# Turning the raw rows as they land and putting the norm's factor in afterwards, with the recurrence's slabs in the order f, i, q, z

## The chip, the cores and the metric

One Trainium2 chip, one of its cores. The metric is the device time of one execution in microseconds (us). The kernel before takes 618.6 us, the median of 3 runs (618.35 to 620.24).

## The reference

A two-layer decoder trunk over 256 tokens of width 1024, all in float32. Each layer is a mixer and a cross attention, each with a residual. The change touches the first mixer, and of it the part A:

```
h = rms_norm(x, ev_norm) @ ev_w_in            # 8 parts of 1024 columns: aq, af, ai, bq, bk, bv, z (2048)
rms_norm(x, g) = x * rsqrt(mean(x*x) + 1e-6) * g
# part A, per head of 128, 8 heads, chunks of 32 tokens
f = lb + (1 - lb) * sigmoid(af);  k = 1 - f
b = cumsum(log f) within a chunk
q_dec = aq * exp(b);  k_inv = k * exp(-b);  k_end = k * exp(b_last - b)
o = causal(q_dec k_inv^T) ai + q_dec s_prev   # s_prev: the state carried from earlier chunks
y = head_rms_norm(o) * silu(z)
```

Part B is softmax attention on bq, bk and bv, with a rotary turn whose angles come from `positions`. Then come the output projection, the cross attention, and the second layer of the same build.

## The kernel before

**Slabs and quarters.** Every weight is cut into slabs of 1024 rows by 512 columns (2 MB). SP loads slab n into one of two raw buffers, once the slab before the last one has been split (`sp.wait_ge(lo_ready, 4 * (n - 1))`). A slab has four quarters. ACT rounds a quarter to `w_hi` and VectorE (DVE) takes the rest, `w_lo = raw - w_hi`. Each has a ring of four quarters. TensorE (PE) multiplies hi by hi, hi by lo and lo by hi: a quarter of a kind "F" slab is 24 matmuls of 256 columns (lines L1506 to L1508, the result has channels on partitions), a quarter of a kind "T" slab is 12 matmuls of 512 columns (L1524 to L1526, the result has tokens on partitions).

**The order is written out by hand in each engine's program.** The call `ahead(n, q)` on ACT and on DVE splits not quarter q of slab n but the one three further on:

```python
def ahead(n, q):
    n, q = divmod(4 * n + q + 3, 4)
    ...
    dve.wait_ge(hi_ready, 4 * n + q + 1)
    dve.tensor_tensor(ring_quarter(w_lo, n, q), raw_quarter(n, q), ...).then_inc(lo_ready, 1)
```

So `ahead(f, 0)` makes quarter 3 of slab f, and `ahead(f, 1)` quarter 0 of the slab after f. PE waits before each quarter until both halves of it are made. The engines take their instructions strictly in order, so a quarter whose `ahead` stands behind other work comes when that work is done.

**The start.** ACT squares the two row tiles of x (L494), DVE makes the mean's reciprocal (L931 to L935), ACT the root (L449), DVE multiplies the rows by it (`norm_rows`, L942), PE turns the result in 16 transposes of 128x128 (`turn_rows`, L1545), ACT writes `xT_hi` with the gain as a scale (L456), and DVE `xT_lo` (L949). The parameters (13 small DMAs into `prm_rows`) are turned by PE (L1554, L1555) and copied by ACT (L498) between them. All projections of the first mixer read `xT_hi` and `xT_lo`.

**Part A** runs twice, for g = 0 and g = 1 (4 heads each), `stage_a(g)`. Its slabs are in the order f, q, i, z (i is of kind T, the others of kind F). In words, for DVE in g = 1: split four quarters while f is multiplied; `forget(1, 0)` and `forget(1, 1)` on the sigmoids; `f_ready`; `ahead(q, 1)`; `gated_a(0)`, which is the end of group 0's output; `ahead(q, 2)` and `ahead(q, 3)`; then wait for ACT's logarithm and run the cumulative sum (L1114) and the chunk subtraction (L1121, `b_ready`); `ahead(i, 0)`, `ahead(i, 1)`; `k_inv` (L1128), `q_dec` (L1133), the carried halves (L1137, L1140). PE multiplies f, q, i, then waits for `k_inv` and `q_dec` (L1590), then z's quarter 0, the carried halves (L1598, L1602), z's 1 and 2, the outputs (L1614), z's 3. In g = 1 a `mean_square_a(0)` (L1571, four matmuls) stands behind the first quarter of f; the second one stands behind the first quarter of stage B.

In g = 0, DVE also computes the rotary angles (`angles`, L1016 to L1039) among the splits, ACT the sine (L537), and DVE sets its signs (`sign_trig`, L1068 and L1069). In g = 1, GpSimd (POOL) makes `y_lo` of group 0 (L379) when ACT has written `y_hi`.

Of the kernel before, what the change touches and what calls it, by code (L numbers as in the profile page):

```python
# [9 lines left out]
I32 = mybir.dt.int32  # L10
# [39 lines left out]
for _g in range(2):  # L50
    SLABS += [("A", "f", "F", _g), ("A", "q", "F", _g), ("A", "i", "T", _g), ("A", "z", "F", _g)]
# [29 lines left out]
def hybrid_trunk(nc, I, out):  # L81
    with ExitStack() as ctx:
# [50 lines left out]
        fgain = wview(1)  # L133
        kx = scan_mask[:, :].rearrange("p (h t) -> p h t", h=4)
# [13 lines left out]
        mem_landed = sem("mem_landed")  # L148
        prm_landed = sem("prm_landed")
# [13 lines left out]
        trig_ready = sem("trig_ready")  # L163
        sumsq = sem("sumsq")
# [126 lines left out]
        def _(sp):  # L291
# [6 lines left out]
            first_quarter(0)  # L298
            for name, rows in PARAM_ROWS:
# [6 lines left out]
                sp.dma_start(prm_rows[r - P * t:r - P * t + rows, t, :], src).then_inc(prm_landed, 16)  # L306
            for q in range(1, 4):
                first_quarter(q)
            for n in range(1, NSLAB):
                if n == 2:  # L310
                    sp.dma_start(const[:], I["shape_constants"]).then_inc(pos_landed, 16)
                    sp.dma_start(W[:, 3, 0:S].bitcast(I32), I["positions"].broadcast_to([P, S])).then_inc(pos_landed, 16)
# [26 lines left out]
        def _(pool):  # L339
# [3 lines left out]
                               pattern=[[-1, P]], channel_multiplier=1).then_inc(masks_ready, 1)  # L343
# [11 lines left out]
            pool.memset(avg[:], 1.0 / P)  # L355
# [51 lines left out]

            keys_carried(0)
# [12 lines left out]
        def _(act):  # L421
# [61 lines left out]

            def y_high(i):
# [5 lines left out]
            act.preload_act_table(ACT.Sqrt)  # L490
            for t in range(T):
# [4 lines left out]
            ahead(-1, 1)  # L496
            act.wait_ge(prm_turned, 1)
            act.activation(prm[:], proj[0][:, 0:N_ROWS], ACT.Copy).then_inc(prm_ready, 1)  # L498
            act.drain()
            xT_high(0, 0, "ev_norm", 0)  # L500
            ahead(-1, 2)
            ahead(-1, 3)
# [16 lines left out]

            def stage_a(g):  # L520
                f, q, i, z = (slab("A", c, g) for c in "fqiz")
                ahead(f, 0)
# [4 lines left out]
                filled(act, f, 0)  # L527
                act.activation(W[:, 0, 0:512], bank(f, 0)[:], ACT.Sigmoid).then_inc(f_sig, 1)
                act.drain().then_inc(free_of(f, 0), 1)
                ahead(f, 3)  # L530
                ahead(q, 0)
                filled(act, f, 1)
                act.activation(W[:, 0, 512:1024], bank(f, 1)[:], ACT.Sigmoid).then_inc(f_sig, 1)
                act.drain().then_inc(free_of(f, 1), 1)
                if g == 0:
# [3 lines left out]
                ahead(q, 1)  # L539
                if g:  # L540
# [12 lines left out]
                ahead(i, 1)  # L553
                ahead(i, 2)
                ahead(i, 3)
                ahead(z, 0)
                v_rows(i)
                ahead(z, 1)
                ahead(z, 2)
                ahead(z, 3)  # L560
# [357 lines left out]
        def _(dve):  # L918
# [63 lines left out]
            ahead(-1, 2)  # L982
            ahead(-1, 3)

            lg = prm[:, PARAM_AT["hgrn_lb_logits"]:PARAM_AT["hgrn_lb_logits"] + 3 * KC].rearrange(
# [869 lines left out]
```

## Time and profile before

| | |
|---|---|
| median of 3 runs | 618.6 us |
| profiled execution | 618.5 us, of which the span from first to last instruction is 616.8 us |
| busy: PE, DVE, ACT, POOL | 586.1, 413.2, 374.3, 43.4 us |
| share of the span that ends last, by engine | PE 66%, DVE 14%, ACT 9% |

Times are microseconds from the first instruction. In a timeline row the first number is the start, the second the time to the end of a merged group, and "x16" the number of instructions in it; in brackets stands how long the engine was idle before it and what released it.

### The profile page before, as it was taken

Reading aid. Unit: us, or ns where it says so; the run is one execution under the profiler, and the core shown is the slowest. Engines: PE = TensorE matmul, PEld = TensorE weight load, DVE = VectorE, ACT = ScalarE, POOL = GpSimd, SP = SyncE. Lnnn points to the kernel's source line nnn. Section 1 sums busy time; section 2 is a strip of 40 time slices with the busy share of each in tenths; the row PEclk is TensorE's granted clock in tenths of the full one; section 3 lists DMA queues with packets and bytes.
Section 4 is the critical chain, followed back from the end, with each engine's and each line's share of the span. In section 5 each row is a group of like instructions: output and inputs, shape, how many; then the busy total and the mean of one; then the engine's idle time right before and its main releaser. Section 6 shows DMA issues by size and latency. Waiting matters only on the chain.

```text
span 616.8 us, 9596 instructions
## 1 busy us (share of the span) xinstructions
PE 586.1 (95%) x3858; PEld 534.1 (87%) x3858; DVE 413.2 (67%) x618; ACT 374.3 (61%) x553; POOL 43.4 (7%) x45
## 2 busy tenths in 40 slices
PE   3999998999999999999999999998989999999984
PEld 3998997999899898889988999997879897888973
DVE  3987378537965884566557782979946962776554
ACT  5864485257267665646657648598357547566662
POOL 4001003001001000100000001131101000100000
PEclk9999999999999999999999999999999999999998
DMA  8747454445535463563336463333333473256101
GB/s 244 248 144 218 141 181 133 140 137 205 159 115 167 150 230 137 180 228 138 137 138 204 156 247 144 137 137 138 136 137 137 145 265 128 101 202 250 38 1 69
DMA packets 51872, 97.83 MB, mean 159 GB/s; under 512 B 1236, under 2 KB 7668, under 8 KB 51828
## 3 DMA queue, kind: packets, MB, share of 16 engines
q1 hardware_dynamic: 51828, 97.22, 46.4%
q8 instruction: 31, 0.51, 0.3%
q14 instruction: 13, 0.11, 0.0%
HBM read 96.16 MB, written 1.05 MB: 158 GB/s over the span
## 4 chain that ended last, share of the span: by engine, by line
PE 66%; DVE 14%; ACT 9%; DVEq 5%; issue 3%; ACTq 2%; DMA 1%; SPq 0%
PE proj L1506 10%; PE proj L1507 10%; PE proj L1508 10%; PE proj L1524 8%; PE proj L1526 8%; PE proj L1525 8%; DVE w_lo L925 5%; PE head L1614 3%; ACT w_hi L434 3%; PE head L1703 1%; ACT xT_hi L456 1%; DVEq L1115 1%; DVE work L1114 1%; DMA x_residual<-in_x_dram 1%; DVE xT_lo L949 1%
## 5 line engine op out<-in xcount | busy, mean ns | idle before, releaser
L925 DVE TENSOR_TENSOR w_lo<-raw_weights,w_hi 128x1024 fp32r<-128x1024 f32 x176 | 221.9, 1274 | 144.2 <-ACT w_hi L434 142.6
L434 ACT ACTIVATE w_hi<-raw_weights 128x1024 fp32r<-128x1024 f32 x176 | 184.1, 1057 | 136.5 <-PE proj L1508 72.5
L1506 PE MATMUL proj<-xT_hi,w_hi 128*128 128x256 f32 x768 | 223.7, 291 | 3.3 <-DVE xT_lo L949 1.7
L1507 PE MATMUL proj<-xT_lo,w_hi 128*128 128x256 f32 x768 | 218.0, 284 | 0.0
L1508 PE MATMUL proj<-xT_hi,w_lo 128*128 128x256 f32 x768 | 218.0, 284 | 0.0
L1506 PEld LDWEIGHTS proj<-xT_hi,w_hi 128*128 128x128 f32 x768 | 148.0, 193 | 6.6 <-issue 5.8
L1507 PEld LDWEIGHTS proj<-xT_lo,w_hi 128*128 128x128 f32 x768 | 148.1, 193 | 1.4 <-issue 1.2
L1508 PEld LDWEIGHTS proj<-xT_hi,w_lo 128*128 128x128 f32 x768 | 147.9, 193 | 0.0
L1524 PE MATMUL proj<-w_hi,y_hi 128*128 128x512 f32 x192 | 76.2, 397 | 0.0
L1526 PE MATMUL proj<-w_lo,y_hi 128*128 128x512 f32 x192 | 74.8, 390 | 0.0
L1525 PE MATMUL proj<-w_hi,y_lo 128*128 128x512 f32 x192 | 74.8, 389 | 0.0
L1524 PEld LDWEIGHTS proj<-w_hi,y_hi 128*128 128x128 f32 x192 | 36.1, 188 | 8.3 <-issue 0.6
L1526 PEld LDWEIGHTS proj<-w_lo,y_hi 128*128 128x128 f32 x192 | 36.0, 188 | 7.6
L1525 PEld LDWEIGHTS proj<-w_hi,y_lo 128*128 128x128 f32 x192 | 36.1, 188 | 7.4 <-issue 0.2
L1524 PE MATMUL proj<-w_hi,xT_hi 128*128 128x512 f32 x96 | 37.9, 394 | 2.3 <-DVE w_lo L925 2.2
L1525 PE MATMUL proj<-w_hi,xT_lo 128*128 128x512 f32 x96 | 37.4, 390 | 0.0
L1526 PE MATMUL proj<-w_lo,xT_hi 128*128 128x512 f32 x96 | 37.4, 390 | 0.0
L379 POOL TENSOR_TENSOR y_lo<-work,y_hi 128x1024 fp32r<-128x1024 f32 x7 | 17.7, 2531 | 274.1 <-ACT y_hi L487 274.1
L1524 PEld LDWEIGHTS proj<-w_hi,xT_hi 128*128 128x128 f32 x96 | 18.0, 188 | 7.1 <-issue 2.6
L1526 PEld LDWEIGHTS proj<-w_lo,xT_hi 128*128 128x128 f32 x96 | 18.0, 188 | 3.9
L1525 PEld LDWEIGHTS proj<-w_hi,xT_lo 128*128 128x128 f32 x96 | 18.1, 188 | 3.4
L949 DVE SCALAR_TENSOR_TENSOR xT_lo<-head,prm,xT_hi 128x256 fp32r<-128x256 f32 x32 | 12.9, 475 | 8.2 <-ACT xT_hi L456 8.2
(237 smaller groups left out, 684.5 us busy)
## 6 DMA issues: line engine op xcount, KB each, us to landing
raw_weights<-in_ev_w_in_dram SPq DMA_DIRECT2D x15, 2048.0 KB, 8.5
raw_weights<-in_od_w_in_dram SPq DMA_DIRECT2D x12, 2048.0 KB, 8.5
raw_weights<-in_ev_w_out_dram SPq DMA_DIRECT2D x4, 2048.0 KB, 8.1
raw_weights<-in_xa_wkv_dram SPq DMA_DIRECT2D x4, 2048.0 KB, 8.4
raw_weights<-in_od_w_out_dram SPq DMA_DIRECT2D x4, 2048.0 KB, 7.7
raw_weights<-in_xa_wq_dram SPq DMA_DIRECT2D x2, 2048.0 KB, 9.0
raw_weights<-in_xa_wo_dram SPq DMA_DIRECT2D x2, 2048.0 KB, 8.3
raw_weights<-in_ev_w_in_dram SPq DMA_DIRECT2D x4, 512.0 KB, 5.6
```

Source lines behind the costliest of these rows:

```text
L379: pool.tensor_tensor(y_lo[:, 4 * G:4 * G + 4, :], y_src(i), y_hi[:, 4 * G:4 * G + 4, :].bitcast(F32), ALU.subtract).then_inc(y_lo_ready, 1)
L434: act.activation(ring_quarter(w_hi, n, q), raw_quarter(n, q), ACT.Copy).then_inc(hi_ready, 1)
L456: act.activation(xT_hi[:, k, :], head[k // 2][:, S * (k % 2):S * (k % 2) + S], ACT.Copy, scale=param(gain, gk + k)).then_inc(xT_hi_ready, 1)
L925: dve.tensor_tensor(ring_quarter(w_lo, n, q), raw_quarter(n, q), ring_quarter(w_hi, n, q).bitcast(F32), ALU.subtract).then_inc(lo_ready, 1)
L949: dve.scalar_tensor_tensor(out=xT_lo[:, k, :], in0=head[k // 2][:, S * (k % 2):S * (k % 2) + S], scalar=param(gain, gk + k), in1=xT_hi[:, ...
L1506: pe.matmul(dst, wh[:, k, :], x_hi[:, k, :], start=(k == 0), stop=False)
L1507: pe.matmul(dst, wh[:, k, :], x_lo[:, k, :], start=False, stop=False)
L1508: last = pe.matmul(dst, wl[:, k, :], x_hi[:, k, :], start=False, stop=(k == KC - 1))
L1524: pe.matmul(dst, x_hi[:, k0 + k, tok], wh[:, k, :], start=first and k == 0, stop=False)
L1525: pe.matmul(dst, x_lo[:, k0 + k, tok], wh[:, k, :], start=False, stop=False)
L1526: last = pe.matmul(dst, x_hi[:, k0 + k, tok], wl[:, k, :], start=False, stop=final and k == 1)
L1614: last = pe.matmul(dst[:, a:a + w], v_sb[:, t, P * h:P * h + P], src, start=(j == 0), stop=(j == len(spans) - 1), skip_group_check=True)
```

## The change

1. The order of the slabs in part A becomes f, i, q, z.
2. PE turns the raw rows of x as they land, after 6 matmuls of the identity by itself. ACT and DVE write the turned rows times the gain into `y_hi` and `y_lo` (`raw_high`, `raw_low`). The first two slabs (f and i of group 0) are multiplied with these. Their results lack the norm's factor. DVE puts it in for f (`scaled_f`, by a row of factors that PE spreads with a matmul of `avg` and a diagonal), ACT for i (`scaled_v_rows`, a scale for each token).
3. POOL splits the second quarter of the first slab (`second_low`) and makes the normed rows (`first_rows`). PE turns these behind the f slab, and `xT_hi` and `xT_lo` are written behind that, for the q slab and later ones.
4. SP loads the gain alone behind the first quarter, then the three other quarters, then the 12 other small rows.
5. Angles, sine and signs move from g = 0 to g = 1, and their scratch space from `work` to `memT`.
6. In `stage_a`, z's quarter 0 comes ahead of the L1590 group, and the outputs come behind z's quarter 3.

The diff's core (DVE and PE; the ACT side follows the same order):

```diff
-    SLABS += [("A", "f", "F", _g), ("A", "q", "F", _g), ("A", "i", "T", _g), ("A", "z", "F", _g)]
+    SLABS += [("A", "f", "F", _g), ("A", "i", "T", _g), ("A", "q", "F", _g), ("A", "z", "F", _g)]
...
             first_quarter(0)
+            small_rows(*PARAM_ROWS[0], gain_landed)
             for q in range(1, 4):
                 first_quarter(q)
+            for name, rows in PARAM_ROWS[1:]:
+                small_rows(name, rows, prm_landed)
...
+            def second_low():
+                pool.wait_ge(hi_ready, 2)
+                pool.tensor_tensor(ring_quarter(w_lo, 0, 1), raw_quarter(0, 1), ...).then_inc(second_lo, 1)
+            def first_rows():
+                pool.wait_ge(rstd_ready, 1)
+                for c in range(2):
+                    for t in range(T):
+                        last = pool.tensor_scalar(mem_rows[:, t, 512 * c:512 * c + 512], ...)
+                    last.then_inc(normed, 1)
...
+            act.preload_act_table(ACT.Sqrt)
+            square_row(0)
+            act.wait_ge(prm_turned, 1)
+            act.activation(prm[:, 0:KC], proj[2][:, 0:KC], ACT.Copy).then_inc(prm_ready, 1)
+            ahead(-1, 1)
+            act.drain()
+            raw_high(range(0, 4))
+            ahead(-1, 2)
+            raw_high(range(4, 8))
+            ahead(-1, 3)
+            square_row(1)
+            act.wait_ge(prm_turned, 2)
+            act.activation(prm[:, KC:], proj[2][:, KC:N_ROWS], ACT.Copy).then_inc(prm_ready, 1)
             root(0)
+            ahead(slab("A", "f", 0), 0)
+            act.wait_ge(rstd_psum, 1)
+            act.activation(rstd_row, proj[3][:, 0:S], ACT.Copy).then_inc(rstd_copied, 1)
...
-            norm_rows(0, x_sb, W[:, 0:2, :])
             ahead(-1, 1)
             dve.wait_ge(prm_ready, 1)
-            xT_low(0, "ev_norm", 0)
-            ahead(-1, 2)
-            ahead(-1, 3)
+            raw_low(range(KC))
+            dve.wait_ge(second_lo, 1)
+            dve.wait_ge(hi_ready, 3)
+            dve.tensor_tensor(ring_quarter(w_lo, 0, 2), raw_quarter(0, 2), ...).then_inc(lo_ready, 2)
+            rstd(0)
...
+            last.then_inc(diag_ready, 1)
+            ahead(slab("A", "f", 0), 0)
+            dve.wait_ge(prm_ready, 2)
...
             def angles():
...
-                ahead(slab("A", "f", 0), 2)
+                ahead(slab("A", "f", 1), 2)
...
-                ahead(slab("A", "f", 0), 3)
+                ahead(slab("A", "f", 1), 3)
...
             def stage_a(g):
+                if g:
+                    ahead(f, 0)
+                    ahead(f, 1)
+                    angles()
+                    forget(g, 0)
+                    ahead(i, 0)
+                else:
+                    ahead(f, 1)
+                    scaled_f(f, 0)
+                    ahead(f, 2)
+                    forget(g, 0)
+                    ahead(f, 3)
+                    scaled_f(f, 1)
+                    ahead(i, 0)
+                forget(g, 1)
...
+                ahead(i, 1)
+                if g:
+                    gated_a(0)
+                    sign_trig()
                 else:
-                    sign_trig()
-                ahead(q, 2)
-                ahead(q, 3)
+                    xT_low(0, "ev_norm", 0)
                 dve.wait_ge(lnf_ready, g + 1)
...
                 last.then_inc(b_ready, 1)
-                ahead(i, 0)
-                ahead(i, 1)
+                ahead(i, 2)
+                ahead(i, 3)
                 dve.wait_ge(exps_ready, 3 * g + 3)
                 dve.tensor_tensor(wview(0), wview(1), wview(0), ALU.mult).then_inc(kinv_ready, 1)
+                ahead(q, 0)
+                ahead(q, 1)
+                ahead(q, 2)
...
+            warm_up(6)
+            for t in range(T):
+                pe.wait_ge(x_landed[t], 16)
+                for k in range(KC):
+                    last = pe.transpose(head[k // 2][...], x_sb[:, t, P * k:P * k + P], ident[:])
+                    if t and k % 2:
+                        last.then_inc(x_turned, 1)
+                if t == 0:
+                    pe.wait_ge(gain_landed, 16)
+                    pe.transpose(proj[2][:, 0:KC], prm_rows[0:KC, 0, :], ident[0:KC, 0:KC]).then_inc(prm_turned, 1)
+            def first_slab(n):
+                quarter_f(n, 0, y_hi, y_lo, raw_x=True)
+                pe.wait_ge(prm_ready, 1)
+                pe.wait_ge(prm_landed, 16 * (len(PARAM_ROWS) - 1))
+                pe.transpose(proj[2][:, 0:P], prm_rows[:, 0, :], ident[:])
...
+                quarter_f(n, 1, y_hi, y_lo)
+                pe.wait_ge(diag_ready, 1)
+                pe.matmul(proj[3][:, 0:S], avg[:], memT[:, 5, :], start=True, stop=True).then_inc(rstd_psum, 1)
+                slab_f(n, [2, 3], x=(y_hi, y_lo))
+                turn_rows(mem_rows, 0)
+                pe.wait_ge(prm_ready, 2)
+                pe.wait_ge(rstd_copied, 1)
...
+                if g:
+                    slab_f(f, [0])
                     mean_square_a(0)
+                    slab_f(f, [1, 2, 3])
+                    slab_t(i)
+                    slab_f(q)
+                else:
+                    first_slab(f)
+                    slab_t(i, x=(y_hi, y_lo))
+                    slab_f(q, norm=0)
+                slab_f(z, [0])
```

## Rows read from the trace of the kernel before

**Rows 1.** Waits of PE in the first 130 us: total, times, longest.
```profile
PE head L1590 <- issue: 1.6, 1, 1.6
PE head L1590 <- DVE work L1133: 0.4, 1, 0.4
```
**Rows 2.** Timeline of PE, from the first slab to stage B.
```profile
18.09 0.32 PE L1506 MATMUL proj<-xT_hi,w_hi 128*128 128x256 f32 x1
...
71.49 1.88 PE L1571 MATMUL head<-work,avg 128*128 128x512 f32 x4
72.80 0.68 PE L1506 MATMUL proj<-xT_hi,w_hi 128*128 128x256 f32 x1
...
93.34 0.40 PE L1524 MATMUL proj<-w_hi,xT_hi 128*128 128x512 f32 x1
...
106.03 2.02 PE L1590 MATMUL head<-work 128*128 128x128 f32 x16 [1.61 <-issue]
...
127.04 1.88 PE L1571 MATMUL head<-work,avg 128*128 128x512 f32 x4
```
**Rows 3.** Timeline of all engines in the first 22 us.
```profile
1.71 0.43 SPq L296 DMA_DIRECT2D raw_weights<-in_ev_w_in_dram  x1
...
6.98 2.54 SPq L296 DMA_DIRECT2D raw_weights<-in_ev_w_in_dram  x3
...
12.13 0.30 ACT L498 ACTIVATE prm<-proj 128x160 f32<-128x160 f32 x1 [3.48 <-PE proj L1555]
12.52 3.03 ACT L456 ACTIVATE xT_hi<-head,prm 128x256 fp32r<-128x256 f32 x8
...
13.48 3.22 DVE L949 SCALAR_TENSOR_TENSOR xT_lo<-head,prm,xT_hi 128x256 fp32r<-128x256 f32 x8 [2.86 <-ACT xT_hi L456]
...
14.11 0.55 PE L1506 MATMUL proj<-xT_hi,w_hi 128*128 128x256 f32 x1 [0.97 <-DVE xT_lo L949]
...
18.89 0.16 DVE L987 TENSOR_TENSOR lbp<-prm 128x8 f32<-128x8 f32 x1
...
21.23 2.36 DVE L925 TENSOR_TENSOR w_lo<-raw_weights,w_hi 128x1024 fp32r<-128x1024 f32 x2
```
**Rows 4.** DMA issues between 1.7 and 2.0 us: size, us to landing.
```profile
raw_weights<-in_ev_w_in_dram SPq DMA_DIRECT2D x1, 512.0 KB, 5.6
```
**Rows 5.** Timeline of PE at the transposes of the memory's rows.
```profile
205.08 1.91 PE L1545 MATMUL head<-ident,shared_rows 128*128 128x128 f32 x16
206.74 0.47 PE L1524 MATMUL proj<-w_hi,xT_hi 128*128 128x512 f32 x1
```
**Rows 6.** Timeline of DVE: the angles in group 0, and group 1.
```profile
23.51 0.29 DVE L1016 CAST work<-work 128x256 f32<-128x256 int32 x1
...
32.53 0.73 DVE L1075 TENSOR_SCALAR work<-work,lbp 128x256 f32<-128x256 f32 x2
...
88.34 1.66 DVE L1083 SCALAR_TENSOR_TENSOR work<-head,prm,work 128x256 f32<-128x256 f32 x4 [1.06 <-ACT work L518]
...
91.22 2.36 DVE L925 TENSOR_TENSOR w_lo<-raw_weights,w_hi 128x1024 fp32r<-128x1024 f32 x2
...
99.14 1.22 DVE L925 TENSOR_TENSOR w_lo<-raw_weights,w_hi 128x1024 fp32r<-128x1024 f32 x1
```
**Rows 7.** Timeline of ACT: the sine in group 0, and the roots in group 1.
```profile
32.65 1.06 ACT L537 ACTIVATE trig<-trig 128x1024 f32<-128x1024 f32 x1 [2.05 <-DVE trig L1039]
...
35.02 2.01 ACT L434 ACTIVATE w_hi<-raw_weights 128x1024 fp32r<-128x1024 f32 x2
...
85.93 1.25 ACT L516 ACTIVATE work<-head,stats 128x512 f32<-128x512 f32 x2
```
**Rows 8.** Two lines by themselves: ns min/median/max, first and last start.
```profile
L1114 DVE TENSOR_TENSOR_SCAN work<-scan_mask,work x2: 2284/3388/4493, 40.1 to 93.5; 128x1024 f32<-128x1024 f32 x2
L379 POOL TENSOR_TENSOR y_lo<-work,y_hi x7: 2404/2415/3088, 92.8 to 529.7; 128x1024 fp32r<-128x1024 f32 x7
```
**Rows 9.** Windows at the end: length, busy of PE, PEld, DVE, ACT, POOL, granted clock, DMA.
```profile
606.00:610.00 4.00, 2.69 (x12) 1.88 (x10) 1.83 (x4) 1.41 (x5) 0.00 (x0) 1.00 0.00 0
612.00:614.00 2.00, 0.00 (x0) 0.00 (x0) 0.66 (x2) 1.16 (x2) 0.00 (x0) 0.52 0.43 158
```

More of the change, by code:

```diff
@@ L133, in hybrid_trunk @@
         fgain = wview(1)
+        rstd_row = memT[:, 4, :]
         kx = scan_mask[:, :].rearrange("p (h t) -> p h t", h=4)
@@ L296, in first_quarter, with small_rows @@
                 sp.dma_start(raw_quarter(0, q), dram_slab(0)[:, :, P * q:P * q + P]).then_inc(first_landed[q], 16)
-            first_quarter(0)
-            for name, rows in PARAM_ROWS:
+            def small_rows(name, rows, landed):
                 src = I[name]
@@ L482, in v_rows, with scaled_v_rows, raw_high @@
                     copy_bank(n, t, v_sb[:, t, :], v_ready)
+            def scaled_v_rows(n):
+                for t in range(T):
+                    filled(act, n, t)
+                    act.activation(v_sb[:, t, :], bank(n, t)[:], ACT.Copy, scale=st[:, 6 + t:7 + t]).then_inc(v_ready, 1)
+                    act.drain().then_inc(free_of(n, t), 1)
+            def raw_high(ks):
+                for k in ks:
+                    if k % 2 == 0:
+                        act.wait_ge(x_turned, k // 2 + 1)
+                    act.activation(y_hi[:, k, :], head[k // 2][:, S * (k % 2):S * (k % 2) + S], ACT.Copy,
+                                   scale=param("ev_norm", k)).then_inc(raw_hi_ready, 1)
             def y_high(i):
@@ L487, in y_high, with square_row @@
                 act.activation(y_hi[:, 4 * G:4 * G + 4, :], y_src(i), ACT.Copy).then_inc(y_hi_ready, 1)
-            act.preload_act_table(ACT.Sqrt)
-            for t in range(T):
+            def square_row(t):
                 act.wait_ge(x_landed[t], 16)
@@ L526, in stage_a @@
                 ahead(f, 2)
[L527 to L529 removed]
+                forget_gate(f, g, 0)
                 ahead(f, 3)
[L531 to L535, printed above, removed]
+                ahead(i, 0)
+                forget_gate(f, g, 1)
+                if g:
                     act.wait_ge(angles_ready, 1)
@@ L552, in stage_a @@
                 act.activation(wview(3), wview(2), ACT.Exp).then_inc(exps_ready, 1)
-                ahead(i, 1)
[L554 to L560, printed above, removed]
+                ahead(q, 0)
+                if g:
+                    v_rows(i)
+                else:
+                    scaled_v_rows(i)
+                for j in range(1, 4):
+                    ahead(q, j)
+                for j in range(4):
+                    ahead(z, j)
                 squares_a(g)
@@ L977, in _, with raw_low @@
             dve.drain()
-            norm_rows(0, x_sb, W[:, 0:2, :])
+            def raw_low(ks):
+                for k in ks:
+                    dve.wait_ge(raw_hi_ready, k - k % 2 + 2)
+                    dve.scalar_tensor_tensor(out=y_lo[:, k, :], in0=head[k // 2][:, S * (k % 2):S * (k % 2) + S],
+                                             scalar=param("ev_norm", k), in1=y_hi[:, k, :].bitcast(F32),
+                                             op0=ALU.mult, op1=ALU.subtract).then_inc(raw_lo_ready, 1)
             ahead(-1, 1)
             dve.wait_ge(prm_ready, 1)
-            xT_low(0, "ev_norm", 0)
-            ahead(-1, 2)
-            ahead(-1, 3)
+            raw_low(range(KC))
+            dve.wait_ge(second_lo, 1)
+            dve.wait_ge(hi_ready, 3)
+            dve.tensor_tensor(ring_quarter(w_lo, 0, 2), raw_quarter(0, 2), ring_quarter(w_hi, 0, 2).bitcast(F32),
+                              ALU.subtract).then_inc(lo_ready, 2)
+            rstd(0)
+            diag = memT[:, 5, :]
+            dve.wait_ge(masks_ready, 1)
+            for t in range(T):
+                last = dve.tensor_scalar(diag[:, P * t:P * t + P], ident[:], st[:, 6 + t:7 + t], float(P),
+                                         ALU.mult, ALU.mult)
+            last.then_inc(diag_ready, 1)
+            ahead(slab("A", "f", 0), 0)
+            dve.wait_ge(prm_ready, 2)
             lg = prm[:, PARAM_AT["hgrn_lb_logits"]:PARAM_AT["hgrn_lb_logits"] + 3 * KC].rearrange(
@@ L1134, in stage_a @@
                                       ALU.mult).then_inc(qdec_ready, 1)
+                    if u == 0:
+                        ahead(q, 3)
                 dve.drain().then_inc(free_of(q, 0), 1)
@@ L1607, in stage_a @@
                 out_a(g)
-                slab_f(z, [3])
             def values_out(h, spans):
```

111 lines of the change are left out of this document (67 added, 44 removed).

## The prediction

> **What bounds the kernel now.** I read the waits of PE first, then its timeline, then DVE and ACT beside it. From the first matmul of a slab at 14.11 [rows 3] PE runs almost without a gap: in the first 130 us its waits behind that are the two ahead of L1590, 0.4 us in group 0 and 1.6 in group 1 [rows 1]. So the end is set by three things: when PE gets its first slab, how much it has to multiply, and where it must wait. An edit on another engine counts only through these.
>
> Lengths used below. A quarter of kind F takes (93.34 - 72.80) / 7 = 2.93 us, the four matmuls of L1571 take 72.80 - 71.49 = 1.3, and the T slab 106.03 - 1.61 - 93.34 = 11.1 [rows 2]. From one L1571 group to the next, 71.49 to 127.04, it is 55.55 us [rows 2]: the length of group 1. ACT splits a quarter in 1.0 [rows 7], DVE in 1.2 [rows 6].
>
> **Part 1: the start and group 0.** Before, squares, root, normed rows, 16 transposes and the parameters all stand ahead of the first matmul at 14.11. After, the first quarter of weights has landed at 1.71 + 5.6 = 7.3 [rows 3, 4], and x was there earlier, since ACT was squaring it. The gain is issued right behind that quarter, and I take it to land with it. Its turn and copy cost 0.3 each (the copy of all parameters took 0.30 [rows 3]): 7.9. ACT's split brings 8.9, DVE's 10.1, and from the first `raw_low` to the first matmul it is 0.63, as from 13.48 to 14.11 [rows 3]. PE starts at about 10.7, so 3.4 us sooner. ACT makes the eight turned pieces at 3.03 / 8 = 0.38 with a split (1.0) in their middle, and DVE follows by about 13.9. PE at its lower clock needs 8 x 0.64 = 5.1 us for the quarter, so this pacing costs some 0.1.
>
> PE gets new work in exchange. The 16 transposes of the normed rows now stand behind the f slab: 206.74 - 205.08 = 1.7 [rows 5]. The two transposes of the parameters cost 0.4 and the `avg` matmul 0.2 (a half of one of L1571's, 1.3 / 4). The wait of 0.4 at L1590 [rows 1] goes, since z's quarter 0 (2.93) now covers it. Sum: -3.4 + 0.1 + 1.7 + 0.4 + 0.2 - 0.4 = -1.4.
>
> DVE must keep up with that. PE asks for quarter 1 of q at 10.7 + 4.7 (quarter 0, partly at the low clock) + 0.4 + 2.93 + 0.2 + 5.9 + 1.7 + 11.1 + 2.93 = 40.5. DVE makes it behind `b_ready`. It has split f's last quarter at about 19.2 (the q2 rounding ends at 14.1, then the second square, 1.2, the root and its steps, 1.0, and a split on each engine). From there it has the lower bound's operations, 2.3 (18.89 to 21.23 [rows 3]), and 0.6 more for ACT's table; five splits, 6.0; two `scaled_f`, 1.3; `forget` twice, 0.73 each [rows 6], and `f_ready`, 0.8; `xT_low`, 3.2 [rows 3]; the scan, 2.3 at its shortest [rows 8], and what follows it, 1.2; then the split itself, 1.2. With 1 us of waits for ACT this gives 19.2 + 21.3 = 40.5. Both arrive together, so I take 0.1 for a slip: **-1.3**, between -2.2 (PE starts a microsecond sooner) and -0.3 (DVE is a microsecond late). Slab 1 is issued later by the 12 small rows, at about 12 instead of 9.6, but the three quarters ahead of it now go out behind the first one instead of at 6.98 [rows 3], so I have it land at 20 as before, and ACT needs it at 21. POOL's split and its normed rows lie beside PE's first slab.
>
> **Part 2: group 1, where the new order puts a split behind the scan.** I count from the first L1571 group, 71.49 = 0. Before, `b_ready` comes at 99.14 - 71.49 = 27.65, and the first split behind it [rows 6] is the last quarter of i, which PE wants at about 30. The two quarters ahead of it were split at 91.22, ahead of the scan [rows 6]. The change takes these two `ahead` calls out from ahead of the scan and puts them behind `b_ready`. Now the last split ahead of the scan is quarter 0 of q. PE comes to quarter 1 of q at 1.3 + 3 x 2.93 + 11.1 + 2.93 = 24.1.
>
> When is `b_ready`? The two splits less (2.3) are made up by what moved in. Angles cost 32.53 - 23.51 - two splits = 6.7 us of DVE [rows 6]. They start behind `ahead(f, 1)`, at about 4, and with two splits in them end at 13. Sine and table take 35.02 - 32.65 = 2.4 of ACT [rows 7], a split 1.0, so the roots start at 16.4 instead of 85.93 - 71.49 = 14.4 [rows 7]. `gated_a` starts as much later, 18.9 instead of 16.85, takes 2.9 [rows 6] and ends at 21.8; signs 0.6; the scan starts at 22.4, where it was 22.0 [rows 8]. From scan to `b_ready` it was 5.6 (93.5 to 99.14), with POOL's `y_lo` beside the scan. Kept so, `b_ready` is at 28.0 and the quarter at 29.2. PE waits 29.2 - 24.1 = 5.1 us. Behind that the splits come every 1.2 us and PE takes 2.93 for each, so there is no second wait. `q_dec` is done 0.7 behind the q slab, and z's quarter 0 covers it: the 1.6 at L1590 goes. Group 1: +5.1 - 1.6 = **+3.5**. With the scan at 2.3, as in group 0 [rows 8], `b_ready` is 2.2 sooner, and it is +1.3. That is the lower bound. The upper one is +4.2, if the sine's load shifts the chain by 0.7 more.
>
> The clock may add to it. After its last matmuls, at about 608.7, PE had nothing, and in 612 to 614 the granted clock was 0.52 [rows 9]: it fell after some 3.4 us. The wait of 5.1 is longer. At the start it took until 18.09 [rows 2] to get from the first slab's matmul at the low level (1.2 GHz) to the high one (2.4): 4 us, in which a matmul took 0.21 instead of 0.12, so 1.7 us lost. I take 1.0 between 0 and 1.7, because the fall may come too late in the gap to happen. The Trainium skill (TensorE: Matmul & The Clock Gate, What's actually happening) says as well that idleness closes the gate and only sustained activity opens it again; by it the full 1.7 would be due whenever the gap closes the gate.
>
> Group 1's other moves lie under cover: `memT` as scratch costs nothing, the outputs behind z's last quarter move ACT's squares by 2.9, still ahead of the next L1571, and stages behind it are as before.
>
> **Sum** against the profiled 618.5 (span 616.8 and 1.7 around it): 618.5 - 1.3 + 3.5 + 1.0 = 621.7. The median is 0.1 above the profiled run: **621.8**.
>
> **The rivals.**
> - *The scan escapes POOL.* It starts before `y_lo` does, since ACT must first write `y_hi` (1.0), and takes 2.3, and the subtraction goes on before POOL takes its turn. For it speaks group 0's 2.28 [rows 8]; against it, that the subtraction has to come through as well. The wait is 2.9, too short for the clock to fall: 618.6 - 1.3 + 1.3 = 618.6, no change. The Trainium skill (SBUF — State Buffer, Who interferes with whom) says that DVE with two SBUF inputs and a GpSimd instruction that reads SBUF exclude each other, and the first to start keeps the ports for its whole length; the 4.49 against 2.28 agrees. By it the scan would run free, and POOL's 2.4 would then hold up the subtraction instead, which comes to the forecast again; only if the subtraction got in first is it this rival. Chance 0.17.
> - *Faster: no wait in group 1.* One mechanism: the chain to `b_ready` in group 1 runs ahead, because it now has two splits less. It decides if `b_ready` is there by 22.9, 5.1 sooner than I have it. Then -1.3 - 1.6: 615.7. Against it: the roots' row and `gated_a` alone reach 21.8. A much sooner start would also do (another 2 us). Chance 0.12.
> - *The start gives nothing back.* The gain lands late, or DVE's chain in group 0 (scaled copies, `xT_low`, blocked operations beside POOL's normed rows) is 2 us later than counted, so q's quarter 1 waits in group 0 too: 621.8 + 1.6 = 623.4. Both meet at 40.5, which speaks for it. Chance 0.12.
>
> **How the numbers follow.** The forecast has 0.59, with its own range 620.2 (clock stays up) to 623.6 (full clock loss, upper bounds). The range of all cases leaves out most of the 0.12 below and a little above: 617.0 to 624.3. Within 0.3% is 616.7 to 620.5, about what a measurement of this kernel can tell from no change. Faster: 0.12 and a tail of the first rival, 0.13. Same: most of the first rival and the forecast's low end, 0.25. Slower: 0.62.
>
> **What would show it.** In the profile after: the first slab matmul near 10.7; L1571 groups 59 to 60 us apart instead of 55.55; PE's longest wait behind the start at a quarter of q in group 1, released by DVE's `w_lo`; matmuls of 0.21 us behind it; no wait at the matmuls of L1590. I am wrong if the split of q's quarter 1 is made before PE has done quarter 0, which a `b_ready` 5 us sooner would do, or if the start is worth more than 3.4 us to PE.

## The result: 1% slower, more than forecast

The changed kernel takes 625.5 us (median of 4 runs, 624.5 to 626.1) against 618.65 us for the kernel before in the same rounds: ratio 1.0094, 95% interval 1.0077 to 1.0112. (Ratios here are those on record; they are close to, but not exactly, the quotient of the two medians, which is 1.011 here.) The forecast was 621.8 with a range up to 624.3, so the sign was right and the size was not: 3.7 us are missing. The profiled execution took 624.5 us with a span of 622.8, where before had 618.5 and 616.8.

The two longest waits of PE in the first 135 us of the changed kernel (total, times, longest); two more, of 1.8 and 1.1 us, also stand ahead of the first slab's work. They answer to [rows 1]:

```profile
PE proj L1613 <- DVE w_lo L993: 5.1, 1, 5.1
PE proj L1674 <- DMA prm_rows<-in_ev_norm_dram: 2.3, 1, 2.3
```

Both waits of [rows 1] are gone, and one of 5.1 has come. (The one of 2.3, for the gain, lies ahead of the first slab.) PE's timeline shows where (the counterpart of [rows 2]; L1613 to L1615 are a quarter of kind F, L1703 is the group that was L1571):

```profile
11.12 0.55 PE L1613 MATMUL proj<-y_hi,w_hi 128*128 128x256 f32 x1 [1.06 <-DVE y_lo L1050]
...
70.59 1.88 PE L1703 MATMUL head<-work,avg 128*128 128x512 f32 x4
...
94.59 0.28 PE L1615 MATMUL proj<-xT_hi,w_lo 128*128 128x256 f32 x1
99.94 0.55 PE L1613 MATMUL proj<-xT_hi,w_hi 128*128 128x256 f32 x1 [5.08 <-DVE w_lo L993]
100.30 0.42 PE L1614 MATMUL proj<-xT_lo,w_hi 128*128 128x256 f32 x1
100.51 0.41 PE L1615 MATMUL proj<-xT_hi,w_lo 128*128 128x256 f32 x1
...
103.70 0.28 PE L1615 MATMUL proj<-xT_hi,w_lo 128*128 128x256 f32 x1
103.82 0.28 PE L1613 MATMUL proj<-xT_hi,w_hi 128*128 128x256 f32 x1
...
131.23 1.88 PE L1703 MATMUL head<-work,avg 128*128 128x512 f32 x4
```

The start and group 0 give 71.49 - 70.59 = 0.9 back. Group 1 takes 131.23 - 70.59 = 60.64 us instead of 55.55: +5.1. Behind the wait the matmuls start 0.21 us apart up to 103.7, and 0.12 from there on. That makes +4.2 at 131 us.

The rest comes 320 us later, in work that the change does not touch. PE's timeline of stage D of the second layer, after and before:

```profile
454.42 4.53 PE L1750 MATMUL head<-shared_rows,v_rows 128*128 128x256 f32 x16 [2.31 <-DVE shared_rows L1523]
458.70 0.36 PE L1613 MATMUL proj<-xT_hi,w_hi 128*128 128x256 f32 x1
```

```profile
450.10 2.86 PE L1614 MATMUL head<-shared_rows,v_rows 128*128 128x256 f32 x16 [2.30 <-DVE shared_rows L1421]
452.71 0.36 PE L1506 MATMUL proj<-xT_hi,w_hi 128*128 128x256 f32 x1
```

The same 16 matmuls behind the same wait of 2.3 us take 4.53 us in place of 2.86, and the next slab starts 6.0 later than before instead of 4.3. Windows of the changed kernel over both places (length; busy of PE, PEld, DVE, ACT, POOL; granted clock; DMA):

```profile
95.00:100.00 5.00, 0.06 (x1) 0.09 (x1) 4.85 (x8) 1.30 (x3) 2.65 (x1) 0.68 0.00 0
100.00:103.00 3.00, 3.00 (x14) 3.00 (x15) 3.00 (x3) 2.85 (x4) 2.10 (x2) 0.50 0.00 0
104.00:105.00 1.00, 1.00 (x10) 1.00 (x10) 0.78 (x1) 0.46 (x2) 1.00 (x2) 1.00 0.66 205
450.00:454.00 4.00, 2.11 (x18) 1.90 (x16) 4.00 (x5) 1.43 (x3) 2.26 (x1) 1.00 0.00 0
454.00:456.00 2.00, 1.58 (x7) 1.38 (x8) 1.42 (x2) 1.77 (x2) 0.00 (x0) 0.81 0.77 182
456.00:458.00 2.00, 2.00 (x8) 1.78 (x7) 1.22 (x2) 0.60 (x1) 0.00 (x0) 0.50 1.04 403
```

The granted clock is 0.50 (1.2 GHz) behind both waits. In group 1 it fell within the wait: a mean of 0.68 over 95 to 100 puts the fall near 96.8, 2.0 us after PE's last matmul, and it was up again near 103.7. In stage D it was still 1.00 through the wait and fell some 0.8 us after PE had gone to work again. So the profiled difference is -0.9 + 5.1 + 1.7 = 5.9, against 6.0 of span.

DVE in group 1 of the changed kernel shows what the 5.1 are made of (the counterpart of [rows 6]; L1213 is the scan, L1220 the subtraction of `b_ready`), with POOL's `y_lo` below it:

```profile
89.83 1.66 DVE L1170 SCALAR_TENSOR_TENSOR work<-head,prm,work 128x256 f32<-128x256 f32 x4 [1.06 <-ACT work L577]
...
93.23 2.28 DVE L1213 TENSOR_TENSOR_SCAN work<-scan_mask,work 128x1024 f32<-128x1024 f32 x1
95.59 2.10 DVE L1217 COPY chunk_sum<-work 128x32 f32<-128x32 f32 x1
97.77 0.90 DVE L1220 TENSOR_TENSOR work<-work,chunk_sum 128x128 f32<-128x128 f32 x4
98.58 2.35 DVE L993 TENSOR_TENSOR w_lo<-raw_weights,w_hi 128x1024 fp32r<-128x1024 f32 x2
```

```profile
93.96 3.69 POOL L395 TENSOR_TENSOR y_lo<-work,y_hi 128x1024 fp32r<-128x1024 f32 x1 [46.10 <-ACT y_hi L536]
```

### The profile page after: what moved, and what is told of

Same layout as the page of the kernel before. It is cut to its first block, busy times and chain, and to the rows that moved or that the text cites. A ratio compares the mean times of both kernels' runs of the same rounds, so it can differ in the third digit from the quotient of the medians.

```text
span 622.8 us, 9685 instructions
## 1 busy us (share of the span) xinstructions
PE 593.7 (95%) x3889; PEld 541.3 (87%) x3889; DVE 418.2 (67%) x625; ACT 377.9 (61%) x563; POOL 58.0 (9%) x50
## 4 chain that ended last, share of the span: by engine, by line
PE 77%; DVE 9%; ACT 6%; DVEq 2%; ACTq 2%; issue 2%; DMA 1%; SPq 0%
PE proj L1613 13%; PE proj L1614 13%; PE proj L1615 13%; PE proj L1631 9%; PE proj L1633 9%; PE proj L1632 9%; PE head L1750 4%; DVE w_lo L993 3%; ACT w_hi L468 2%; PE head L1839 1%; DMA prm_rows<-in_ev_norm_dram 1%; PE head L1652 1%; ACT xT_hi L490 1%; DVE v_rows L1444 1%; PE head L1727 1%
## 5 line engine op out<-in xcount | busy, mean ns | idle before, releaser
L1613 PE MATMUL proj<-xT_hi,w_hi 128*128 128x256 f32 x736 | 214.8, 292 | 7.5 <-DVE w_lo L993 6.8
L1614 PE MATMUL proj<-xT_lo,w_hi 128*128 128x256 f32 x736 | 208.8, 284 | 0.0
L1615 PE MATMUL proj<-xT_hi,w_lo 128*128 128x256 f32 x736 | 208.8, 284 | 0.0
L1613 PEld LDWEIGHTS proj<-xT_hi,w_hi 128*128 128x128 f32 x736 | 141.7, 193 | 11.1 <-issue 10.3
L1614 PEld LDWEIGHTS proj<-xT_lo,w_hi 128*128 128x128 f32 x736 | 141.9, 193 | 1.5 <-issue 1.2
L1615 PEld LDWEIGHTS proj<-xT_hi,w_lo 128*128 128x128 f32 x736 | 141.7, 193 | 0.0
L1631 PE MATMUL proj<-w_hi,y_hi 128*128 128x512 f32 x208 | 82.5, 397 | 0.0
L1631 PE MATMUL proj<-w_hi,xT_hi 128*128 128x512 f32 x80 | 31.6, 395 | 2.2 <-DVE w_lo L993 2.2
L1613 PE MATMUL proj<-y_hi,w_hi 128*128 128x256 f32 x96 | 28.5, 296 | 1.1 <-DVE y_lo L1050 1.1
L1614 PE MATMUL proj<-y_lo,w_hi 128*128 128x256 f32 x96 | 27.9, 291 | 0.0
L1615 PE MATMUL proj<-y_hi,w_lo 128*128 128x256 f32 x96 | 27.8, 290 | 0.0
L1613 PEld LDWEIGHTS proj<-y_hi,w_hi 128*128 128x128 f32 x96 | 19.2, 200 | 1.8 <-issue 1.7
```

The lines of the kernel that those rows point to most:

```text
L1613: pe.matmul(dst, wh[:, k, :], x_hi[:, k, :], start=(k == 0), stop=False)
L1614: pe.matmul(dst, wh[:, k, :], x_lo[:, k, :], start=False, stop=False)
L1615: last = pe.matmul(dst, wl[:, k, :], x_hi[:, k, :], start=False, stop=(k == KC - 1))
L1631: pe.matmul(dst, x_hi[:, k0 + k, tok], wh[:, k, :], start=first and k == 0, stop=False)
```

## The experiments

Groups and times are those of each kernel's profiled execution. "Fill" is a multiplication of the identity by itself into a bank that the next group overwrites; it changes no result.

**Turn the chain round (scan_first).** Group 1 runs logarithm, scan and subtraction right behind the forget gates; the roots, `gated_a`, the signs and `y_high` come behind.

```diff
@@ DVE, g = 1
                 ahead(i, 1)
-                gated_a(0)
-                sign_trig()
                 dve.wait_ge(lnf_ready, g + 1)
                 ... scan, b_ready
                 ahead(i, 2)
                 ahead(i, 3)
+                gated_a(0)
                 ... k_inv
                 ahead(q, 0)
                 ahead(q, 1)
                 ahead(q, 2)
+                sign_trig()
```

> The changed kernel, with group 1's chain turned round: logarithm, scan and subtraction come straight behind the forget gates, and the roots, group 0's gated output and the signs come behind them, so the splits of q's quarters 1 and 2 are made by about 93.5 and 94.7 where PE wants them at 94.7 and 97.6. Theory A (the split behind the scan makes the wait): no wait of PE in group 1, the two L1703 groups 54.0 us apart instead of 60.6, about 616.2 us, or 617.9 if the clock still falls at the wait of 2.3 us in stage D. Rival B (the later cost is not this wait, but the new order or the new start as such): at least 621. Rival C (the clock's falls have nothing to do with the long wait): the clock still falls once in group 1.

Measured 619.0 us (12 runs, 617.0 to 621.3), ratio 0.9997 (0.9982 to 1.0013). Its DVE timeline in group 1:

```profile
88.66 2.29 DVE L1210 TENSOR_TENSOR_SCAN work<-scan_mask,work 128x1024 f32<-128x1024 f32 x1
91.02 0.19 DVE L1214 COPY chunk_sum<-work 128x32 f32<-128x32 f32 x1
91.28 0.90 DVE L1217 TENSOR_TENSOR work<-work,chunk_sum 128x128 f32<-128x128 f32 x4
92.10 2.35 DVE L993 TENSOR_TENSOR w_lo<-raw_weights,w_hi 128x1024 fp32r<-128x1024 f32 x2
```

The quarter is split 6.5 us sooner, PE does not wait for it, the clock stays up in group 1, and the L1703 groups are 125.65 - 70.57 = 55.08 apart (a wait of 1.15 at L1727, the former L1590, is left). The whole loss of group 1 came from that one wait. The copy takes 0.19 with POOL idle and 2.10 beside it. The time is 1.1 above the 617.9 expected with a fall in stage D (the profile has that fall): the wait of 1.15 at L1727 was not foreseen. The 12 runs lie 4.3 us apart, so they stand on several steps.

**Fill the wait (filled_gap, filled_22).** 44, then 22 fills stand between quarters 0 and 1 of q in group 1, so that PE is busy while it waits.

```diff
-                    slab_f(q)
+                    slab_f(q, [0])
+                    pe.wait_ge(y_ready, 1)
+                    for _ in range(44):      # 22 in filled_22
+                        pe.matmul(head[3][:, 0:P], ident[:], ident[:], start=True, stop=True)
+                    slab_f(q, [1, 2, 3])
```

> The changed kernel with 44 multiplications of the identity by itself put into PE's wait of 5.1 us ahead of q's quarter 1 in group 1; their result is used nowhere. Theory A (the wait costs 3.5 net, and the clock's fall in it 1.6 more): the quarter still starts at about 99.9, but the matmuls behind it come every 0.12 us at once, and the time is 1.6 us less than the changed kernel's. Rival (the slow matmuls do not lie on the path, since DVE's splits set the pace there): no change. Either way the wait of 2.3 us in stage D comes at another distance from the start, and its fall of the clock may or may not come again.

> As the run with 44 multiplications in the wait, but with 22, since each takes two steps of the array and 44 of them ran 4.4 us past the end of the wait. Theory A: they end about when the split does, the clock stays up in group 1, the two L1703 groups are 59.0 us apart (60.6 in the changed kernel), and the time is 1.6 us under the changed kernel's. Rival (the clock's fall there costs nothing on the path): 60.6 apart, no change.

44 were too many: they held PE until 103.87, and the kernel took 627.0 us (6 runs, ratio 1.0114), 1.5 over the changed kernel and not 1.6 under it as expected. But the clock did not fall in group 1, and from the first matmul behind the fill to the next L1703 group it was 133.54 - 103.87 = 29.67, where the changed kernel has 131.23 - 99.94 = 31.29. With 22 the wait is just covered: 623.2 us (4 runs, 622.8 to 623.5), ratio 1.0063, and

```profile
70.95 1.88 PE L1703 MATMUL head<-work,avg 128*128 128x512 f32 x4
...
129.97 1.88 PE L1703 MATMUL head<-work,avg 128*128 128x512 f32 x4
```

59.02 apart in place of 60.64. Both give the same price for the fall in group 1: 1.6 us. The low clock lasted about 6.8 us there, of which 3.1 fell into the wait and cost nothing.

**Old order in group 1 (old_order_g1).** Slabs f, q, i, z there; the splits stay where the change put them, for the slabs in this sequence. On ACT `v_rows` of i also moves back, behind one more split.

```diff
-for _g in range(2):
-    SLABS += [("A", "f", "F", _g), ("A", "i", "T", _g), ("A", "q", "F", _g), ("A", "z", "F", _g)]
+SLABS += [("A", "f", "F", 0), ("A", "i", "T", 0), ("A", "q", "F", 0), ("A", "z", "F", 0)]
+SLABS += [("A", "f", "F", 1), ("A", "q", "F", 1), ("A", "i", "T", 1), ("A", "z", "F", 1)]
```

> The changed kernel, but in group 1 with the slabs in the order of before (f, q, i, z), while the splits keep their new places: two of them behind the chunk subtraction. Theory A (the place of the splits decides, not the order of the slabs): PE waits at quarter 1 of the third slab (now i) about 5 us, and the time is that of the changed kernel within 1 us. Rival (the order decides): the wait is under 2 us and the time 620 or less.

Measured 625.2 us (4 runs), ratio 1.0095 (1.0075 to 1.0115), the changed kernel's time. The wait is there again, now ahead of a quarter of i; the second row is a wait in group 0, at 41.42 (PE's waits):

```profile
PE proj L1634 <- DVE w_lo L995: 4.6, 1, 4.6
PE proj L1616 <- DVE w_lo L995: 1.0, 1, 1.0
```

So the order of the slabs does not make the wait; what stands ahead of the splits does. That the time agrees so well is partly luck. In this profile the groups were 133.08 - 71.08 = 62.00 apart, 1.4 more than in the changed kernel: the clock fell near 99.7, only 0.7 us before PE resumed at 100.42, and was back near 106.5, so nearly the whole low stretch fell on work. Against that, the clock did not fall in stage D, where the 16 matmuls took 2.86.

**Without the angles (no_angles).** Angles, sine and signs are left out and the table is a constant, so the rotary turn is left out of the result.

```diff
-                    act.activation(trig[:], trig[:], ACT.Sin).then_inc(trig_ready, 1)
 def angles():
-                pos = memT[:, 1, :] ... (24 lines of VectorE work)
                 ahead(slab("A", "f", 1), 2)
                 ahead(slab("A", "f", 1), 3)
```

> The changed kernel without the rotary angles, their sine and their signs in group 1; the angles' table is filled with a constant, so the rotary turns are left out of the result. It takes 6.7 + 0.6 us off DVE and 2.3 off ACT ahead of the scan. Theory A (the roots started 2.0 later through them and the signs stood ahead of the scan, the rest is the place of the splits): the scan starts 2.6 us sooner, the wait is 2.5 instead of 5.1, the clock stays up in group 1, about 4.2 us less than the changed kernel. Rival (the angles are the whole cause): no wait in group 1, 616 us. Rival (they are no part of it, the mean square sets the roots): no change.

Measured 620.8 us (10 runs), ratio 1.002 (1.0004 to 1.0035). The wait in group 1 shrank from 5.08 to 2.23, so the moved angles are worth 2.9 us of it. The time, 4.7 under the changed kernel's, is near the expected 4.2, but one part of the expectation was wrong: the clock did fall in group 1. The groups are 129.26 - 71.61 = 57.65 apart, where scan_first's length without its wait, 53.93, and the wait of 2.23 make 56.2: a price of 1.5. Stage D made up for it, since in this profile the clock did not fall there. The windows around the wait of 95.89 to 98.12:

```profile
96.00:98.00 2.00, 0.00 (x0) 0.00 (x0) 2.00 (x6) 1.12 (x3) 0.00 (x0) 1.00 0.00 0
98.00:100.00 2.00, 1.88 (x14) 1.91 (x15) 2.00 (x2) 2.00 (x4) 0.92 (x1) 0.88 0.00 0
100.00:102.00 2.00, 2.00 (x11) 2.00 (x11) 1.40 (x2) 1.72 (x3) 1.68 (x4) 0.50 0.00 0
```

A wait of 2.2 us brought the fall as well, some 1.4 us after PE had gone to work again. The same run had PE wait 1.55 us in group 0 at 40.41, for DVE's split of a slab that had landed at 23.0.

**Fill stage D alone (before_filled_d, after_filled_d).** Ten fills in the wait of 2.3 us ahead of the former L1614, in the kernel before and in the changed one.

```diff
+                if g == 0:
+                    pe.wait_ge(att_ready, 9)
+                    for _ in range(10):
+                        pe.matmul(head[0][:, 0:P], ident[:], ident[:], start=True, stop=True)
                 pe.wait_ge(v_ready, 10 + 2 * g + 2)
```

> The kernel before with 10 multiplications of the identity by itself in PE's wait of 2.3 us in stage D, their result used nowhere. The runs of the kernel before stand on three steps, 618.5, 620.2 and 621.4 us, at mean clocks 0.997, 0.994 and 0.991. Theory D (the steps are falls of the clock after that wait, which happen in some runs and not in others, in either kernel): the clock doesn't fall there any more, and most runs are at 618.5, median 1.6 us under the kernel before. Rival E (the falls come from elsewhere): the steps stay and the median is the same.

> The changed kernel with only the 10 multiplications in stage D's wait of 2.3 us. Theory (the profiled run of the changed kernel has 1.7 us from a fall of the clock there, as many runs of the kernel before have too, and the rest of the loss is group 1's wait with its own fall): 624.5 - 1.7 = 622.8 us, and the median at 623 to 624, since a fall near 591 can still come. Rival (the changed kernel makes stage D slower in itself): the L1750 group there still takes 4.5 instead of 2.9 us, 625.5.

The changed kernel falls from 625.5 to 623.1 us (4 runs, 622.9 to 623.3; ratio 1.0054, 1.0039 to 1.007) and its 16 matmuls are back at

```profile
454.49 2.86 PE L1750 MATMUL head<-shared_rows,v_rows 128*128 128x256 f32 x16
```

The kernel before goes from 620.17 (median of 29 runs on that chip: 11 of them at 618.5 to 619.4, 15 near 620.2, 3 near 621.4) to 618.75 (12 runs, nine of them at 618.5 to 618.8, none over 620.04). Its ratio, 0.9993 (0.9983 to 1.0004), cannot be told from 1; what went is the share of runs on the upper steps: 18 of 29 without the fill, 3 of 12 here, and 3 of 12 in before_scan_first, which has the fill too. So this wait was already there, and in some runs of before it very likely already cost a step of 1.65 us. The one profile of before itself has no such fall, so this is argued from times.

The other profiles say whose fall it is. Seven executions have the wait without the fill, of 2.30 or 2.31 us each. Three of them, from scan_first, filled_22 and no_angles:

```profile
448.81 4.53 PE L1750 MATMUL head<-shared_rows,v_rows 128*128 128x256 f32 x16 [2.31 <-DVE shared_rows L1523]
453.14 4.33 PE L1754 MATMUL head<-shared_rows,v_rows 128*128 128x256 f32 x16 [2.30 <-DVE shared_rows L1523]
452.39 2.86 PE L1722 MATMUL head<-shared_rows,v_rows 128*128 128x256 f32 x16 [2.31 <-DVE shared_rows L1495]
```

The clock fell in four (the changed kernel, scan_first, filled_gap, filled_22) and not in three (before, no_angles, old_order_g1). In the six profiles with the fill it never fell there. So the changed kernel does not make stage D slower in itself: where the clock stays up its 16 matmuls take 2.86, as before.

**The chain turned round in the kernel before (before_scan_first).** Start and slab order of before, group 1 as in scan_first, stage D filled.

```diff
@@ DVE, g = 1, slab order f, q, i, z
-                gated_a(0)
-                ahead(q, 2)
-                ahead(q, 3)
                 dve.wait_ge(lnf_ready, g + 1)
                 ... scan, b_ready
+                ahead(q, 2)
+                ahead(q, 3)
                 ahead(i, 0)
+                gated_a(0)
```

> The kernel before, with its old start and its old order f, q, i, z, but with group 1's chain turned round as in the first experiment (scan and subtraction straight behind the forget gates), and with the 10 multiplications in stage D. Theory F (the new start is worth the 0.9 us that the profile shows and no more, and the wait of 1.6 at L1590 in group 1 comes from the late scan): no wait at L1590 in group 1, 618.5 - 1.6 = 616.9 with no fall of the clock, as good as or better than the changed kernel with the chain turned round. Rival (the new start is needed for it): over 618.

Measured 618.4 us (12 runs), ratio 0.9986 (0.9976 to 0.9997): a miss of 1.5 us. PE's waits show why:

```profile
PE head L1595 <- issue: 1.4, 1, 1.4
PE head L1595 <- DVE work L1138: 1.2, 1, 1.2
```

The 1.4 is group 1's, where before had 1.6 [rows 1]: a sooner `b_ready` does not take this wait away. `gated_a` now stands ahead of `q_dec`, which may be why; I did not test it. The 1.2 is group 0's, which the edit does not touch and where before had 0.4; it is no part of the miss. In this execution the first slab's matmuls came 0.12 us apart from the start, and group 0 still ended at 71.49, as in before. What PE gained there it waited away at L1595, for DVE's `work`: in group 0 DVE's chain and not PE's start set the end.

**A sooner start (gain_first, early_rows, both_filled).** All have the chain turned round and stage D filled. gain_first issues the gain ahead of x. early_rows also moves the 12 small rows from SP's queue to ACT's. both_filled is gain_first with 2, 4 and 2 fills in three waits of the last cross attention.

```diff
@@ SP, gain_first
+            small_rows(*PARAM_ROWS[0], gain_landed)
             for t in range(T):
                 sp.dma_start(x_sb[:, t, :], I["x"][0][P * t:P * t + P, :]).then_inc(x_landed[t], 16)
             first_quarter(0)
-            small_rows(*PARAM_ROWS[0], gain_landed)
@@ ACT, early_rows
+            for name, rows in PARAM_ROWS[1:]:
+                small_rows(act, name, rows, prm_landed)
             act.preload_act_table(ACT.Sqrt)
```

> The changed kernel with the chain turned round and the 10 multiplications in stage D, and with the gain's row issued by SP ahead of x instead of behind the first quarter of weights, and turned ahead of x. Theory (the missing 0.4 us at the start, a first slab matmul at 11.1 instead of 10.7, is the wait of 2.3 us for the gain up to 7.9): the gain's transpose no longer waits behind the x rows, ACT rounds the first quarter when it lands, at about 7.6, and the first slab matmul comes at about 10.5. Whether group 0 ends sooner is open: DVE's chain meets PE at q's quarter 1 (39.6 and 37.9 + 2.9), so at most 0.3 us come through. Rival (weights' landing sets it too): 11.1 again. Time with no fall of the clock 616.3 to 616.9.

> The changed kernel with the chain turned round, the 10 multiplications in stage D, the gain's row issued ahead of x and turned first, and the 12 other small rows issued on ACT's queue instead of SP's. Theory G (in the changed kernel the gain's landing sets the first matmul, and the 12 issues delay slab 1, whose landing at 22.0 holds DVE's chain in group 0): no wait of 2.3 us ahead of the gain's transpose, the first slab matmul about 0.5 sooner (then it waits for the first quarter of weights), slab 1 lands by 19, and group 0 ends 0.5 to 1 us sooner: 615.5 to 616.0 us with no fall of the clock. Rival (DVE's own work is the bound in group 0, whatever lands when): 616.6.

> The run with the gain first, and in the last cross attention 2, 4 and 2 multiplications of the identity by itself in PE's waits of 0.5, 0.95 and 0.5 us ahead of the transposed probabilities, into a bank that is free there. In other runs the clock fell at about 591 to 593, behind these waits. Theory D (short waits before it decide about the fall): it comes no more, and nearly all runs are at the lowest step, 616.5 us, 1.6 or more under the kernel before's median of 620.2. Rival (falls there have another cause): the steps of 1.6 us stay as in the run without them.

Medians of 12 runs each: gain_first 618.1 (ratio 0.9985, 0.9972 to 0.9999), early_rows 617.9 (0.9969, 0.9957 to 0.9981), both_filled 617.8 (0.9971, 0.996 to 0.9982). All three missed what was expected of them (616.3 to 616.9, 615.5 to 616.0, and 616.5). None clearly brought the first matmul of a slab forward: it came at 12.42, 11.34 and 10.83. The changed kernel had 11.12, and the six other profiled executions with its start (scan_first, filled_gap, filled_22, no_angles, old_order_g1, after_filled_d) had 10.67 to 11.13. The gain was turned at 4.67 instead of 7.94, but ACT then waited for the first quarter of weights. SP's queue in gain_first, ACT's first two splits and slab 1's first split:

```profile
2.10 7.27 SPq L304 DMA_DIRECT2D raw_weights<-in_ev_w_in_dram  x4
9.56 1.06 ACT L468 ACTIVATE w_hi<-raw_weights 128x1024 fp32r<-128x1024 f32 x1 [3.79 <-DMA raw_weights<-in_ev_w_in_dram]
12.14 1.07 ACT L468 ACTIVATE w_hi<-raw_weights 128x1024 fp32r<-128x1024 f32 x1
...
15.07 0.42 SPq L340 DMA_DIRECT2D raw_weights<-in_ev_w_in_dram  x1
25.27 2.01 ACT L468 ACTIVATE w_hi<-raw_weights 128x1024 fp32r<-128x1024 f32 x2 [2.45 <-DMA raw_weights<-in_ev_w_in_dram]
```

Four issues took SP 7.3 us in this execution and 5.6 in both_filled's, with the same instructions. Here slab 1 landed only at 25.3, and PE waited 2.15 us for its split at 42.0 in group 0. In early_rows slab 1 was issued at 8.2 and the split at 21.58 did not wait; group 0 ended 0.2 us sooner than in scan_first (70.34 against 70.57). The extra fills of both_filled brought a median that can't be told from gain_first's; its 12 runs lie closer together (617.3 to 618.7 against 617.4 to 621.0). The best of these is 0.3% under the kernel before.

## Why the forecast was right in kind and wrong in size

**Start and group 0: forecast -1.3, measured -0.9.** The first slab matmul came at 11.12 and not at 10.7: the gain was turned at 7.94, and its copy and the first split ended at 9.3, not at 8.9. The next L1703 group came at 70.59 against a forecast 70.2. One execution decides less than this seems to: in the seven profiles with this start the first matmul came at 10.67 to 11.13 and the L1703 group at 70.01 to 71.61, so the start was worth 1.5 us in the best of them and nothing in the worst, against 71.49 in before. "Both arrive together" held: DVE split quarters 1 and 2 of q from 39.58, and PE started quarter 0 at 37.93. "I have it land at 20" did not: slab 1 was issued at 13.0 and landed at 22.0, since the three quarters ahead of it kept SP from 2.71 to 7.37 and 12 rows followed. It was in time here, but not in every execution (no_angles, old_order_g1, gain_first).

**Group 1's wait: forecast 5.1, measured 5.08.** The place, the releaser and the length are as worked out: quarter 1 of q, by DVE's `w_lo`, with the split behind `b_ready`. The wait at L1590 went, as forecast, but that z's quarter 0 covers it is not shown: in scan_first, where PE is not held up earlier, a wait of 1.15 stands there. In one part the way to `b_ready` was another: I had the scan slowed by POOL, but it began first (93.23 against 93.96) and took 2.28, and the copy behind it took 2.10. The sum was the same. The Trainium skill (SBUF — State Buffer, Who interferes with whom), by which the first to start keeps the ports and the other waits, describes this order, and both traces agree: before, POOL was first and the scan took 4.49 [rows 8]. That it was the small copy and not the subtraction that POOL held up was in nobody's sum.

**The clock: forecast +1.0, between 0 and 1.7, measured +1.6 in group 1.** Nearly the full price was due: filled_22 and filled_gap give 1.62 each. This term was too small by 0.6. The doubt that halved it was that the fall may come too late; it came 2.0 us into the wait, where [rows 9] had shown 3.4. For the same reason the first rival's "2.9, too short for the clock to fall" does not hold: it fell for a wait of 2.23 in no_angles.

**The step that failed is "stages behind it are as before".** The work was as before; its clock was not. The fall in stage D cost the profiled execution 1.7 us, and no term stood for it. In the one profile of before the clock was up in stage D, so its rows could not show that the clock sometimes falls there. That before's runs lay between 618.35 and 620.24 was in front of me, and I took 620.24 for scatter; it is one step of 1.65 us.

A second term failed beside it: "the median is 0.1 above the profiled run" was 1.0. The 3.7 us missing from the forecast are thus 0.4 (start), 0.6 (clock in group 1), 1.7 (stage D) and 0.9 (median), which make 3.6; the rest is rounding. The stated range was also narrower than its parts: the upper bounds of the start, of group 1 and of the clock add up to 624.2, not to the 623.6 given for the forecast's own range. With the wait of stage D filled in both kernels, the change costs 623.1 - 618.75 = 4.35 us; the parts that belong to it sum to -0.9 + 3.5 + 1.6 = 4.2.

The rivals: that the scan escapes POOL was true of the scan alone and gave nothing, since the copy was caught. That there is no wait in group 1 is what scan_first makes, not the change. That the start gives nothing back came true for single executions, when slab 1 landed late (no_angles, 71.61).

**What stays open.** Why the clock falls in stage D in some executions and not in others, I can't say: the wait and the work around it are the same. It seems to have fallen in all 4 runs of the changed kernel (the slowest with the fill is 1.2 us under the fastest without), but only one of them has a profile. Nor did I find the place of the other 1.0 us in the median. It is not all clock: the run of 625.31 has a higher mean clock than the profiled one of 624.5 (0.986 against 0.983). The scatter of the start could give as much, which no run here shows. A fall stood at one other place too, in the last cross attention (near 591 us in early_rows, 593 in before_scan_first, 601 in filled_gap), behind three waits of only 0.5, 0.95 and 0.5 us.

## What to carry to other kernels

When a split or load is moved behind a chain, work out the chain's end and the consumer's time for it from one origin; here that gave 5.1 us where 5.08 came, and the cure was to run the chain sooner (619.0, no better than the kernel before), not to put the slabs back. Price every wait of TensorE of 2 us or more with a possible fall of the clock, here 1.5 to 1.7 us and more where the whole low stretch falls on work (old_order_g1), and look over the whole kernel for waits that long, whether the change touches them or not. If the runs of a kernel stand on steps and not around a mean, find out what a step is before you use their median.

## What the hardware showed that was not expected

- A fall of the clock to 1.2 GHz followed waits of 2.2 us (no_angles, group 1) and 2.3 us (stage D, in 4 of 7 profiles; in the other 3 the same wait brought none). Against PE's return to work it came anywhere from 0.4 us before it (stage D of filled_22) to 1.4 us behind it (no_angles), and 2.0 us into the wait of 5.1.
- The rows of before give a granted clock of 1.00 from the first microsecond, though its matmuls came 0.21 us apart up to 18.09, the spacing that goes with 0.50 in the changed kernel. So the mean clock can be compared between runs of one kernel, but not between these two kernels.
- Runs of one kernel stand on steps: for before, 618.5 us at a mean granted clock of 0.997, 620.2 at 0.994 and 621.4 at 0.991, some 1.6 us for 0.003.
- A COPY of 128x32 on DVE took 2.10 us beside POOL's 128x1024 operation, and 0.19 without it.
- 44 multiplications of a 128x128 float32 identity count as 88 instructions and took 9.99 us: 0.11 for an instruction, 0.23 for a multiplication.
- Four issues of 512 KB on one queue took SP 5.6 to 7.3 us, so what is queued behind them starts that much later, and by another amount in each execution.
